# Prompt attention in 256-query blocks of two heads abreast with V stationary, and decode with one K and one V page per step

## The reference

```python
q, k, v, logf = fox_proj(xn, attn_w_in, attn_b_f)          # 16 heads of 64
# prompt
c = cumsum(logf, axis=1)
s = einsum('bqhd,bkhd->bhqk', q, k) * scale                 # scale = 1/8
s = s + c[query] - c[key]                                   # forget terms, causal mask
o = einsum('bhqk,bkhd->bqhd', softmax(where(causal, s, -inf)), v)
# requests
kp, vp = cache_k[page_table], cache_v[page_table]           # 8 pages of 128 rows each
lp = cache_logf[page_table]
s = einsum('bqhd,bkhd->bhqk', q, concat(kp, k)) * scale + forget terms
o = einsum('bhqk,bkhd->bqhd', softmax(s), concat(vp, v))
```

## Time and profile before

| | |
|---|---|
| median of three runs | 3260.32 us |
| the profiled execution, its own time | 3277.89 us |
| its span, first to last instruction | 3276.1 us |
| mean granted clock of TensorE | 0.934 of 2.4 GHz |
| TensorE busy | 2939.1 us, 90% |
| VectorE, ScalarE, GpSimd busy | 1095.4, 924.1, 782.6 us |
| prompt attention | about 1652 to 2077 us |
| decode | about 2077 to 2342 us |

### The profile page before, as it was taken

One profiled execution on the slowest core, in us unless ns is written; L12 is line 12 of the kernel. 1 busy time (PEld: TensorE's weight loads), 2 busy tenths in 40 slices (PEclk: granted clock), 3 DMA queues, 4 the chain that ended last, 5 costly groups with the idle time before them and its releaser, 6 DMA issues.

```text
span 3276.1 us, 49541 instructions
## 1 busy us (share of the span) xinstructions
PE 2939.1 (90%) x18658; PEld 2725.1 (83%) x18658; DVE 1095.4 (33%) x1876; ACT 924.1 (28%) x1533; POOL 782.6 (24%) x378
## 2 busy tenths in 40 slices
PE   5786698999999999999999999777799999999997
PEld 4786497999999998899977777555688999999997
DVE  5899634111111114411135445433332111111114
ACT  4555533211111113211124334322223212111123
POOL 2899423222221213311200000000022222222221
PEclk8888799999999999999969779978899999999998
DMA  3101011111111111234102001477411111111111
GB/s 93 39 26 33 19 45 33 40 50 45 36 49 37 53 40 50 73 86 113 42 24 74 20 19 45 167 253 275 151 39 39 37 53 39 44 45 37 53 35 69
DMA packets 243435, 206.63 MB, mean 63 GB/s; under 512 B 18188, under 2 KB 218892, under 8 KB 243076
## 3 DMA queue, kind: packets, MB, share of 16 engines
q1 hardware_dynamic: 230215, 186.66, 18.5%
q10 hardware_dynamic: 13133, 18.80, 1.7%
HBM read 183.16 MB, written 23.13 MB: 63 GB/s over the span
## 4 chain that ended last, share of the span: by engine, by line
PE 51%; issue 32%; POOL 8%; DVE 6%; ACT 2%; DMA 1%; DVEq 0%; ACTq 0%; SPq 0%; POOLq 0%
PE PS L673 17%; PE PS L675 16%; PE PS L674 16%; POOL yp L629 7%; DVE tm L1511 2%; POOL wlo L606 1%; DVE rs L1490 1%; DMA xin<-in_x_prompt 1%; DVE hlo L1553 1%; PE PS L800 0%; DVE xlo L1496 0%; ACT prods L1240 0%; ACT tm L1282 0%; ACT xhi L1138 0%; DVE yn L1884 0%
## 5 line engine op out<-in xcount | busy, mean ns | idle before, releaser
L673 PE MATMUL PS<-xhi,whi 128*128 128x352 f32 x3456 | 1144.8, 331 | 134.0 <-DVE u L1605 54.2
L675 PE MATMUL PS<-xlo,whi 128*128 128x352 f32 x3456 | 1121.7, 325 | 0.0
L674 PE MATMUL PS<-xhi,wlo 128*128 128x352 f32 x3456 | 1121.4, 324 | 0.0
L606 POOL TENSOR_TENSOR wlo<-wraw,whi 128x1024 fp32r<-128x1024 f32 x208 | 497.9, 2395 | 1867.0 <-ACT whi L1127 1867.0
L673 PEld LDWEIGHTS PS<-xhi,whi 128*128 128x128 f32 x3456 | 657.9, 190 | 177.8 <-DVE u L1605 56.1
L674 PEld LDWEIGHTS PS<-xhi,wlo 128*128 128x128 f32 x3456 | 661.0, 191 | 0.0
L675 PEld LDWEIGHTS PS<-xlo,whi 128*128 128x128 f32 x3456 | 658.9, 191 | 0.0
L1127 ACT ACTIVATE whi<-wraw 128x1024 fp32r<-128x1024 f32 x208 | 218.9, 1052 | 593.1 <-PE PS L675 565.1
L1548 DVE TENSOR_TENSOR ht<-PS,ht 128x352 f32<-128x352 f32 x132 | 69.1, 524 | 906.7 <-PE PS L675 902.7
L673 PE MATMUL PS<-hhi,whi 128*128 128x352 f32 x1056 | 341.2, 323 | 8.8 <-issue 8.8
L674 PE MATMUL PS<-hhi,wlo 128*128 128x352 f32 x1056 | 338.5, 321 | 0.0
(11 more groups left out here) (184 smaller groups left out, 2386.9 us busy)
## 6 DMA issues: line engine op xcount, KB each, us to landing
wraw<-in_ffn_w_gu SPq DMA_DIRECT2D x88, 512.0 KB, 3.7
kr<-in_cache_k SPq DMA_DIRECT2D x64, 512.0 KB, 6.5
vr<-in_cache_v SPq DMA_DIRECT2D x64, 512.0 KB, 8.1
wraw<-in_ffn_w_down SPq DMA_DIRECT2D x32, 384.0 KB, 3.0
wraw<-in_attn_w_in SPq DMA_DIRECT2D x24, 512.0 KB, 3.8
wraw<-in_ffn_w_down SPq DMA_DIRECT2D x32, 320.0 KB, 2.8
wraw<-in_conv_w_in SPq DMA_DIRECT2D x16, 512.0 KB, 3.9
wraw<-in_conv_w_out SPq DMA_DIRECT2D x8, 512.0 KB, 3.5
```

Of the source, the lines that this page charges most:

```text
L606: nc.gpsimd.tensor_tensor(wlo[:, s, :], wraw[:, s, :], whi[:, s, :].bitcast(F32), ALU.subtract).then_inc(w_lo, 1)
L673: nc.tensor.matmul(out, wh, hi[:, k, blk(b)], start=(k == 0), stop=False)
L674: nc.tensor.matmul(out, wl, hi[:, k, blk(b)], start=False, stop=False)
L675: m = nc.tensor.matmul(out, wh, lo[:, k, blk(b)], start=False, stop=(k == kc - 1))
```

## The change

**Projection.** ScalarE rounds each staged query and key unit to a high part `sth`, GpSimd subtracts for the low part `stl` (`staged_lows`), and both go to scratch: queries as rows high, high, low; keys as rows low, high and two rows with the high and low part of the forget term. VectorE's next staging waits for GpSimd, not for the store.

**Prompt attention.** A score is two FP32R products: `qa` (high, high) by `kau`/`kal` (low, high) over 128 rows, and `qb` (low, with two rows of ones) by `kbu`/`kbl` (high, with the forget rows) over 66 rows. The mask is a third product, the identity by `cmaskr`. Tiles of two heads alternate, longest first (query tiles 7 to 0). Four buffers of `pr` exist; the transposes stand three tiles behind. GpSimd divides the probabilities by the row sum before the transposes. ScalarE copies out bank 4, VectorE bank 5: for long tiles key blocks 1 to 4 and 5 to 8, for short ones head 0 and head 1. Four tiles (two heads, 256 queries) form a block; V is the stationary operand for 256 columns of probabilities, head h writes partitions 64h to 64h + 63, and the result is `OT` as it stands. All 128 tiles are written out on each engine. Keys of the lower half have two buffers; the rest of a pair's data is reloaded as it comes free. The probabilities use the memory of `stg` and `ktok`, so that attention starts after their stores, and the first K pages and the output weights are fetched after it.

**Decode.** Keys run 13 pages ahead of values, and every page step has one of each. Transposes of probabilities move to page 4 of the next request, values span the two requests after, `select` moves to page 7. ScalarE issues the loads of sums and does the exponentials of request b-1 inside request b. SyncE's order is K page n, V page n - 13.

The diff, cut to its core:

```diff
+        def tile(g):
+            i, t = g // NTAU, g % NTAU
+            return i, t % 2, NT - 1 - t // 2
+
+        def uses(g):
+            qt = tile(g)[2]
+            return (True, True) if qt >= 4 else (g % 2 == 0, g % 2 == 1)
+
+        NA = [0]
+        ND = [0]
+        for g in range(TILES):
+            NA.append(NA[g] + uses(g)[0])
+            ND.append(ND[g] + uses(g)[1])
+
+        def block_of(n):
+            return n // 4, NT // 2 - 1 - n % 4
+
+        def block_probs(n):
+            return pta if n % 2 == 0 else ptb
+
+        def portions(n):
+            kts = list(range(2 * block_of(n)[1] + 2))
+            a, e = (len(kts) + 1) // 3, (2 * len(kts) + 1) // 3
+            return [kts[0:a], kts[a:e], kts[e:]]
+
+        LAG = NPG + 5
...
+            for n in range(4, NP + LAG):
+                if n < NP:
+                    load_k(n)
+                if n >= LAG:
+                    load_v(n - LAG)
+                if n == 2 * NPG:
+                    load_pairs(Q_ATTN_OUT, 1, attn_w_out[0], 0, C, two)
...
+            for g in range(TILES):
+                i, h, qt = tile(g)
+                pool.wait_ge(a_rec, g + 1)
+                probs = pr[:, g % 4, 0:(qt + 1) * P]
+                nc.gpsimd.tensor_scalar(probs, probs, rden[:, g % NTAU:g % NTAU + 1], None, ALU.mult).then_inc(a_nrm, 1)
...
+            def prompt_scores(g):
+                i, h, qt = tile(g)
+                t = g % NTAU
+                if t == 0:
+                    pe.wait_ge(a_up, 128 * (i + 1))
+                    pe.wait_ge(a_key[i % 2], 32 * (i // 2 + 1))
+                if t == 8:
+                    pe.wait_ge(a_low, 32 * (i + 1))
+
+                past(pe, a_exp, g - 1)
+                nk = (qt + 1) * P
+                q1, q2 = qa[:, h, qt * P:(qt + 1) * P], qb[:, h, qt * P:(qt + 1) * P]
+                for k0 in range(0, nk, HALF):
+                    n = min(nk - k0, HALF)
+                    out = PS[:, 2 * (g % 2) + k0 // HALF, 0:n]
+                    k1, k2 = (kau[:, h, 0:n], kbu[:, h, 0:n]) if k0 else (kal[:, i % 2, h, 0:n], kbl[:, i % 2, h, 0:n])
+                    last = k0 + n == nk
+                    nc.tensor.matmul(out, q1, k1, start=True, stop=False)
+                    nc.tensor.matmul(out, q2, k2, start=False, stop=not last)
+                m = nc.tensor.matmul(PS[:, 2 * (g % 2) + qt // 4, (qt % 4) * P:(qt % 4 + 1) * P], identr[:, :],
+                                     cmaskr[:, :], start=False, stop=True)
+                m.then_inc(a_sc, 1)
+
+            def probs_tr(g):
+                i, h, qt = tile(g)
+                pe.wait_ge(a_nrm, g + 1)
+                if uses(g)[0]:
+                    past(pe, a_pta, NA[g])
+                if uses(g)[1]:
+                    past(pe, a_ptd, ND[g])
+                for kb in range(qt + 1):
+                    bank = 4 + kb // 4 if qt >= 4 else 4 + g % 2
+                    m = nc.tensor.transpose(PS[:, bank, (kb % 4) * P:(kb % 4 + 1) * P],
+                                            pr[:, g % 4, kb * P:(kb + 1) * P], ident[:, :])
+                    if kb in (3, qt):
+                        m.then_inc(a_tra if bank == 4 else a_trd, 1)
+
+            def prompt_values(n, part):
+                i, bn = block_of(n)
+                if part == 0:
+                    pe.wait_ge(a_pta, NA[4 * n + 4])
+                    pe.wait_ge(a_ptd, ND[4 * n + 4])
+                    past(pe, o_ev, n - 1)
+                for kt in portions(n)[part]:
+                    c0 = P if kt == 2 * bn + 1 else 0
+                    for h in range(2):
+                        m = nc.tensor.matmul(PS[DH * h:DH * h + DH, 6 + n % 2, c0:QW],
+                                             Vt[:, kt, (2 * i + h) * DH:(2 * i + h + 1) * DH],
+                                             block_probs(n)[:, h, kt, c0:QW], start=(kt == 0),
+                                             stop=(kt == 2 * bn + 1), skip_group_check=True)
+                if part == 2:
+                    m.then_inc(a_pv, 1)
+
+            for g in range(TILES + 6):
+                if g < TILES:
+                    prompt_scores(g)
+                if g >= 7:
+                    n, part = divmod(g - 7, 4)
+                    if part < 3:
+                        prompt_values(n, part)
+                if 3 <= g < TILES + 3:
+                    probs_tr(g - 3)
...
+            def request(b, age):
                 for j in range(NPG):
                     page_tr(b, j)
-                    if j == 0 and selects:
-                        pe.wait_ge(d_s, b * 4)
-                        select(b - 2)
-                    if values and j in (1, 2):
-                        if j == 1 and selects:
-                            pe.wait_ge(d_o, b * 2 - 2)
-                        exp_tr(b - 1, j - 1)
+                    if j <= 4 and age >= 2:
+                        values_page(b - 2, j + 3)
+                    if j == 4 and age >= 1:
+                        if age >= 3:
+                            pe.wait_ge(d_o, b * 2 - 4)
+                        exp_tr(b - 1, 0)
+                        exp_tr(b - 1, 1)
                     if j == 5:
                         scores(b, 0)
                     if j == 6:
-                        if values:
+                        if age >= 1:
                             pe.wait_ge(pt_ev, b * 5)
                         new_scores(b)
-                    if j >= 3 and values:
-                        values_page(b - 1, j - 3)
+                    if j >= 5 and age >= 1:
+                        values_page(b - 1, j - 5)
...
+            def store_staged(q, s, keys):
+
+                u = (q - Q_ATTN_IN) * 2 + s
+                past(act, stg_st[s], (q - QK) * 32 + 24 * C if keys else (q - Q_ATTN_IN) * 48)
                 act.wait_ge(ev[s], seen(s, q, NB - 1))
+                nc.scalar.activation(sth[:, s, :], stg[:, s, 0:SEQ], ACT.Copy).then_inc(qk_hi, 1)
+                heads = ds(q * 4 + (2 * s - 4 * (QK if keys else Q_ATTN_IN)), 2)
+                scr, hi_rows, lo_row = (k_scr, (DH,), 0) if keys else (q_scr, (0, DH), P)
+                act.wait_ge(qk_hi, u + 1)
                 act.nop(nofuse=True)
-                act.dma_start(scr[ds(q * (2 * P) + (s * P - q0 * 2 * P), P), :], stg[:, s, 0:SEQ]
-                              ).then_inc(stg_st[s], 16)
-
-            with act.Fori(Q_ATTN_IN, QK) as q:
+                for r in hi_rows:
+                    act.dma_start(scr[heads, r:r + DH, :], sth[:, s, :].bitcast(F32)).then_inc(stg_st[s], 16)
+                act.wait_ge(qk_lo, u + 1)
+                act.nop(nofuse=True)
+                act.dma_start(scr[heads, lo_row:lo_row + DH, :], stl[:, s, :].bitcast(F32)).then_inc(stg_st[s], 16)
...
+            def prompt_exp(g):
+                i, h, qt = tile(g)
+                nk = (qt + 1) * P
+                act.wait_ge(a_max, g + 1)
+                if g >= 4:
+                    if uses(g - 4)[1]:
+                        act.wait_ge(a_trd, ND[g - 4] + 1)
+                    else:
+                        act.wait_ge(a_tra, NA[g - 4] + 1)
+                t = g % NTAU
+                nc.scalar.activation(pr[:, g % 4, 0:nk], banks(2 * (g % 2), nk), ACT.Exp,
+                                     bias=nmx[:, t:t + 1], accum_out=den[:, t:t + 1]).then_inc(a_exp, 1)
+
+            act.wait_ge(cb_st, 16 * NREQ)
+            act.wait_ge(out_st, 16 * 3)
+            for s in range(2):
+                act.wait_ge(kt_st[s], 16 * C // 2)
+            for g in range(TILES + 3):
+                if g >= 3 and uses(g - 3)[0]:
+                    probs_out(g - 3)
+                if g < TILES:
+                    prompt_exp(g)
...
+                    if age and j == 0:
+                        sample_exp(b - 1)
+                        load_sums(b)
+                    if age and j == 4:
+                        sample_probs_out(b - 1, range(5))
...
+            dve.wait_ge(cb_st, 16 * NREQ)
+            for g in range(TILES + 6):
+                if g < TILES:
+                    prompt_max(g)
+                if 1 <= g <= TILES:
+                    prompt_rec(g - 1)
+                if 3 <= g < TILES + 3 and uses(g - 3)[1]:
+                    probs_out(g - 3)
+                if g >= 10 and (g - 10) % 4 == 0:
+                    outputs_out((g - 10) // 4)
...
+            def request(b, age):
+                key_out(b, 1)
                 queries(b)
-                for j in range(1, NPG, 2):
-                    key_out(b, j)
-                    if j == 1 and selects:
-                        to_features(b - 2)
-                    if j == 3 and values:
-                        sums_rec(b - 1)
-                    if j == 5:
-                        score_sums(b, 0)
+                key_out(b, 3)
+                if age >= 2:
+                    sample_out(b - 2)
+                if age >= 1:
+                    sums_rec(b - 1)
+                key_out(b, 5)
```

(62 more changed lines are left out.)

365 lines of the change are left out of this document (153 added, 212 removed).

## The result

The changed kernel took **3371.24 us** (median of four runs, 3362.25 to 3375.64), the kernel before 3255.45 in the same session (3225.69 to 3261.3): 1.0371 times the time, 95% interval 1.0303 to 1.0439. The prediction was 3082 us, and faster with a chance of 0.95. The profiled execution of the changed kernel took 3375.64 us, with a span of 3373.9.

A forecast was written before the change was run, and what follows sets the result against it. TensorE was taken to set the pace in attention, no single thing in decode. Profiled 3277.9 - 148 (attention) - 31 (decode) = 3099 us, by the same offset 3082 for the median; range 3030 to 3165.

The forecast's parts named there:

- Price 0; without that cover 16 x 3.4 = 55: Projection: added high and low parts and stores cost nothing, as TensorE needs the weights only a unit later; otherwise 55 us.
- the fourth: Rival in attention: GpSimd's scaling by a per-row factor sets the pace and the kernel turns slower, 3332 us; chance 0.04.
- 148 forecast: Prompt attention: the stage falls from 425 to 277 us, 148 us won, 140 to 181 by the clock alone.
- the two bounds: Attention, V products per pair at full clock: 15.4 us if the two heads run in turn, else 7.7, which was taken.
- 29 forecast: Attention, one pair of heads at full clock: 25.9 us of TensorE plus 2.2 and 1 of waits, 29 us.
- 14 forecast, 8 to 21.5 as bounds: Attention, GpSimd's scaling of 9216 columns per pair: 14 us taken between 8 and 21.5, all under TensorE's 25.9.
- the two-input row: Earlier profile row used for GpSimd's scaling in attention: a two-input operation takes 2.39 us for 1024 columns, 2.33 ns each.
- +3 us: Attention's start: the first maximum and exponential wait until the eight scratch stores have landed, 3 us more.
- 33 us of the 277: Attention's clock allowance: 244 us at full clock became 277, taken between 269 and 285 for time at 1.2 GHz.
- the low clock: Rival in attention: the clock stays at 1.2 GHz throughout, stage 412 us, whole 3216; chance 0.10.
- 31 forecast: Decode: requests 26 us apart instead of 31.3 win 37 us, less 3 and 2.5 lost; net 31 won, 0 to 50.
- 20.9 + 2.4: Decode, DMA time per request: 20.9 us for 8.4 MB at 402 GB/s, some 2.4 for the broadcast of sums; 23 together.

## Why the prediction was wrong

**Projection: the step that failed.** "Price 0; without that cover 16 x 3.4 = 55". The prediction counted the added stores by their bytes ("the DMA share is 0.30") and by the work of ScalarE and GpSimd, and never by their form. A mean share over 16 engines says nothing for a transfer that only two of them carry. The stage came out 247.6 us longer, 236 of it by the width of these stores: ScalarE's issues stood behind two DMA engines, and the weights' high parts behind ScalarE. The step's cover was real: with split stores 11.5 us are left, well under the 55. With split stores the whole is 3135 us, 53 above the forecast and inside the range given. No rival named the issue of a DMA as something that can hold ScalarE for 29 us; the fourth, the only one on this side, put the danger in the wrong stage.

**Attention: 148 forecast, 131 measured.** The mechanism held. Records of the V products start in twos, 0.02 us apart, and the next two 0.22 later: below, 12 records of 256 columns end in 1.52 us, little over half of what four passes one after another would take (3 key blocks x 2 heads x 256 x 4 / 2.4 GHz = 2.6). Over the pair from 1988.56 they fill 9.6 us (each record counted up to the start of the next), against 7.7 and 15.4 for the two bounds:

```profile
1988.45 0.65 PE L1033 MATMUL PS<-ptb,Vt 128*64 128x256 f32 x4
...
1998.65 1.52 PE L1033 MATMUL PS<-pta,Vt 128*64 128x256 f32 x12
```

So two run at a time, as the earlier trace rows had it for four column groups. That these are the two heads, and not the two records of one product, is not shown: no run has a product 64 columns wide by itself. What was mis-sized is the pair, 29 forecast and 34.2 measured:
- Products: scores 13.0 instead of 10.3 (among them the mask products, 0.18 each for the forecast's 0.11), V 9.6 instead of 7.7, transposes 8.0 as forecast; 30.5 for 25.9. The other 3.7 us are waits, 3.2 forecast.
- GpSimd's scaling: 14 forecast, 8 to 21.5 as bounds, 27.5 measured, 0.28 us and 2.5 ns a column:

```profile
L713 POOL TENSOR_SCALAR pr<-pr,rden 128x1024 f32<-128x1024 f32 x16 | 45.3, 2843 | 69.3 <-DVE rden L1873 69.3
...
L713 POOL TENSOR_SCALAR pr<-pr,rden 128x128 f32<-128x128 f32 x16 | 9.6, 603 | 17.9 <-DVE rden L1873 17.3
```

It is slower per column than the two-input row that was taken for its upper end, and just under the 29 us from which the fourth rival would decide. It did not become the bound, and cost 2.1 us of a pair.

And the start: "+3 us" for the wait on the scratch stores; VectorE stood 13.9 us, TensorE 13.6, and moving the wait won 10.

The clock gave part back: 33 us of the 277 were for it, midway between a third of the stage and its first 60 us at 1.2 GHz. Measured were 0.96 in the stage, which is some 23 us at 1.2 GHz and an estimated price of 10, and 1.00 from 1960 to the end:

```profile
1960.00:2191.00 231.00, 205.71 (x1466) 149.65 (x1466) 135.38 (x326) 122.26 (x296) 184.40 (x112) 1.00 0.29 86
```

So the low clock is out as a cause of the loss. That chance went the good way, and hid some half of the pair's error (8 x 5.2 = 42 us). So the 131 is nearer to the 148 than the working deserved.

**Decode: 31 forecast, 19 measured.** Loads of sums start at 2194.34 for request 0 and at 2391.89 for request 7, so requests lie 28.2 us apart, forecast 26. The 31.3 before counts to the last request's fourth load; from first load to first load it is (2294.70 - 2077.38) / 7 = 31.0 (first fence). 7 x (31.0 - 28.2) makes 20, the 19 measured. In the changed kernel (second fence) one gap lasts 34.9 us, with the output weights' high parts in it; the last four have a mean of 27.0:

```profile
2077.38 2.74 SPq L523 DMA_DIRECT2D cbx<-cb_scr  x4
...
2294.70 2.61 SPq L523 DMA_DIRECT2D cbx<-cb_scr  x4
```

```profile
2249.02 1.28 ACTq L1543 DMA_DIRECT2D cbx<-cb_scr  x2
...
2283.90 1.44 ACTq L1543 DMA_DIRECT2D cbx<-cb_scr  x2
...
2391.89 1.42 ACTq L1543 DMA_DIRECT2D cbx<-cb_scr  x2
```

Windows of 10 us still swing up to 2281, between 180 and 365 GB/s; from there to 2401 they lie between 272 and 383, at a mean share of 0.94, and leaving the sums out wins time, so the DMA engines bound that part:

```profile
2281.00:2401.00 120.00, 97.13 (x1251) 66.04 (x1250) 49.77 (x64) 37.74 (x64) 0.83 (x1) 0.93 0.94 330
```

The sum "20.9 + 2.4" for them is off by the second term: pages alone take 21.2, the sums 6.

**By the signs listed:** pairs 29 us apart: no, but under the 37 called wrong. V records in twos: yes. GpSimd busy 100 to 170 us: no, 220. A chain of waits through GpSimd: a short one, 15.4 us of TensorE's transposes in the stage. Requests 26 apart in windows that don't swing: nearly, in the second half. A clock under 0.7 in attention: no. None of the listed signs looked at the projection.

## What to carry to other kernels

Cost an added DMA by its pattern before its bytes: write down the outermost dimension of both sides, and treat the engines that it leaves as a server of their own, to which every spread transfer in the same time also goes. Its price is small while that server keeps up (here 11.6 us or less for 16 stores) and everything beyond, and it is paid by whatever stands behind the issue, here ScalarE's weights. A stage that the diff "only adds a little to" needs a rival and a sign too.

The version with split stores, shared scaling and the late wait is the fastest that was compared with another in its own session: 3117.73 us, 4.6% under the kernel before (3.8 to 5.4%); with the sums in four copies it was 3108.55 in another session, a difference that these can't settle.

## What was not expected of the hardware

- An issue of a DMA held ScalarE for 17.15 us and SyncE for 16 us a load (two in 32.00), while the DMA share was 0.13.
- Beside a load of 256 KB of sums the rate of full page traffic fell from 409 to 214 GB/s for 8 us, at a DMA share of 1.03. A request lost 6 us to these loads, and other widths and rows changed its distance by 0.6 us at most.
- A TENSOR_SCALAR with a per-row factor takes GpSimd 2.8 us for 1024 columns, the TENSOR_TENSOR of the earlier trace rows 2.4.
